# A hybrid encoder layer on one core: two small parameter loads issued later, zeroing and copies placed elsewhere, the way-in steps redistributed

## The reference, cut to what matters

```python
q, k, v, u, g_a, g_s = split(rms_norm(h) @ w_in)
# attention: 4 heads, two score maps per head
p = softmax(einsum('bqhcd,bkhcd->bhcqk', rope(q), rope(k)) * 64 ** -0.5)
w = p[:, :, 0] - lam * p[:, :, 1]
o_a = rms_norm(w @ v) * (1 - lambda_init)
# S5, both directions, 32 groups of 64 states, 16 channels each
bb = coef * (b_re + i b_im)          # discretised input matrix
x_t = ab * x_{t-1} + bb @ u_t        # scan over 256 steps
y = Re((c_re + i c_im) @ x) + d * u
```

## Time and profile before

| | |
|---|---|
| Median of 3 runs | 1339.34 us (1339.18 to 1340.71) |
| The profiled execution's own time | 1338.22 us |
| Its span in the profile | 1336.3 us |
| TensorE (PE) matmul busy | 1264.0 us (95%) |
| TensorE weight load (PEld) busy | 569.2 us (43%) |
| VectorE (DVE) busy | 373.2 us (28%) |
| ScalarE (ACT) busy | 202.1 us (15%) |
| GpSimd (POOL) busy | 111.2 us (8%) |
| Read from HBM over the span | 454.11 MB, 341 GB/s |
| Mean granted TensorE clock | 0.987 of full speed |

### The profile page before, as it was taken

The page is one execution under the profiler, slowest core; times in us unless marked ns, Lnnn a source line. Parts: engine busy times, 40 slices in busy tenths (PEclk is TensorE's granted clock), DMA queues, the critical chain, the costliest instruction groups (busy, mean ns, idle before and its releaser), DMA issues.

```text
span 1336.3 us, 15275 instructions
## 1 busy us (share of the span) xinstructions
PE 1264.0 (95%) x6167; PEld 569.2 (43%) x6167; DVE 373.2 (28%) x797; ACT 202.1 (15%) x311; POOL 111.2 (8%) x109
## 2 busy tenths in 40 slices
PE   7998899999898999999999999999999999999997
PEld 3477776777743333333333333333333332333332
DVE  6389675022123211122111211112211111221112
ACT  2121252101310111111111111111111111111111
POOL 4499110010001000000000000000000000000000
PEclk8999899999998999999999999999999999999999
DMA  8643375347954999999999999999999999999995
GB/s 229 175 133 126 102 89 175 127 158 283 354 222 167 412 427 429 428 427 428 427 429 427 429 428 429 430 427 429 427 429 430 427 430 428 428 430 427 430 427 218
DMA packets 55128, 456.83 MB, mean 342 GB/s; under 512 B 4760, under 2 KB 6880, under 8 KB 30512
## 3 DMA queue, kind: packets, MB, share of 16 engines
q1 hardware_dynamic: 51744, 449.74, 81.8%
q0 software_dynamic: 2192, 5.99, 2.7%
q10 hardware_dynamic: 1152, 0.52, 0.3%
HBM read 454.11 MB, written 1.61 MB: 341 GB/s over the span
## 4 chain that ended last, share of the span: by engine, by line
PE 62%; DMA 30%; DVE 4%; ACT 2%; issue 1%; SPq 0%; ACTq 0%; DVEq 0%
PE pt L872 17%; DMA ring<-in_w_e 16%; PE pt L912 12%; PE pt L487 7%; DMA stage<-in_w_e 6%; DMA low<-in_w_e 6%; PE pt L474 6%; PE pt L522 4%; PE pt L839 3%; PE pt L826 3%; PE pt L454 3%; PE pt L535 2%; DMA stage<-in_w_in 1%; PE pt L878 1%; ACT wi_ L950 1%
## 5 line engine op out<-in xcount | busy, mean ns | idle before, releaser
L872 PE MATMUL pt<-ring,hres 128*64 128x512 f32 x1216 | 273.1, 595 | 15.2 <-DMA ring<-in_w_e 14.9
L872 PEld LDWEIGHTS pt<-ring,hres 128*64 128x64 f32 x1216 | 84.0, 137 | 198.6 <-issue 167.0
L912 PE MATMUL pt<-ring,wi_ 128*64 128x512 f32 x640 | 141.7, 595 | 5.4 <-ACT wi_ L950 5.4
L1549 DVE TENSOR_SCALAR hnt<-pt 128x512 f32<-128x512 f32 x32 | 22.1, 692 | 308.2 <-PE pt L872 308.2
L1495 DVE COPY ct_<-ct_ 128x2 f32 (+1 forms) x33 | 5.6, 169 | 363.6 <-PE pt L872 359.1
L872 PE MATMUL pt<-stage,hres 128*64 128x512 f32 x416 | 93.9, 595 | 6.7 <-DMA stage<-in_w_e 6.7
L872 PE MATMUL pt<-low,hres 128*64 128x512 f32 x416 | 93.8, 595 | 5.0 <-DMA low<-in_w_e 5.0
L1110 ACT ACTIVATE hnt<-hnt 128x512 f32<-128x512 f32 x32 | 20.2, 630 | 477.8 <-DVE hnt L1549 477.8
L912 PEld LDWEIGHTS pt<-ring,wi_ 128*64 128x64 f32 x640 | 44.5, 137 | 89.7 <-issue 82.4
L839 PE MATMUL pt<-big,lamb 64*128 64x512 f32 x256 | 63.6, 615 | 0.7 <-ACT big L950 0.7
L474 PE MATMUL pt<-stage,hnt 128*128 128x512 f32 x128 | 58.9, 622 | 4.5 <-DMA stage<-in_w_in 4.5
(11 more groups left out here) (314 smaller groups left out, 1265.9 us busy)
## 6 DMA issues: line engine op xcount, KB each, us to landing
ring<-in_w_e SPq DMA_DIRECT2D x116, 2048.0 KB, 40.1
low<-in_w_e SPq DMA_DIRECT2D x38, 2048.0 KB, 41.0
stage<-in_w_e SPq DMA_DIRECT2D x38, 2048.0 KB, 40.0
stage<-in_w_in SPq DMA_DIRECT2D x16, 1024.0 KB, 5.6
stage<-in_w_xkv SPq DMA_DIRECT2D x8, 1024.0 KB, 5.5
stage<-in_w_mix_out SPq DMA_DIRECT2D x4, 1024.0 KB, 5.0
stage<-in_w_xq SPq DMA_DIRECT2D x4, 1024.0 KB, 5.1
stage<-in_w_xo SPq DMA_DIRECT2D x4, 1024.0 KB, 16.3
```

What stands on the lines that cost most here:

```text
L872: last = pe.matmul(pt[PC][SLOTS * g:SLOTS * (g + 1), 512 * b:512 * (b + 1)], xT[:, k % 4, k // 4], ring_slot[n][:, c:c + 512], start=(k == ...
L912: last = pe.matmul(pt[PD][SLOTS * h:SLOTS * (h + 1), 512:1024], hT[:, c, g], ring_slot[n][:, D * c + 512 * h:D * c + 512 * (h + 1)], start ...
L1549: dve.tensor_scalar(hg, pt[PC][:, 0:512], GATE_MAX, None, ALU.min).then_inc(m_g2, 1)
```

## The change

C is loaded only when the second half of slab "u" has landed, and B only when the second half of "q" has. The clears of `bsplit` and of the k halves move up behind the first norm; the rotation's temporaries move from `t3` to a free part of `ring`. The four copies into `bsplit` move from VectorE to ScalarE, behind its copy of the regrouped u. The scaling of the second map in `weigh` moves to ScalarE, behind the exponentials of its head; VectorE signals the factors (`wsc`) and waits for each scaled tile (`wsv`). The way-in steps of VectorE are t = 0 before head 0, 1 after head 0, 2 after head 1, 3 and 4 after head 2. The chunk factors come after head 3. `turn_probs(3)` comes after the second of the eight groups of way-in transposes.

```diff
@@ -371,12 +371,14 @@
                            T["norm_ffn_g"].rearrange("a (j p r) -> p (a j) r", p=P, j=W1_CHUNKS)).then_inc(s_par, 16)
 
             pool.wait_ge(S["graw"], 1)
+            pool.wait_ge(s_slot[1], 16)
             for c, n in enumerate(("ssm_c_re", "ssm_c_im")):
                 for d in range(2):
                     dst = craw[:, c, :, d * NS:(d + 1) * NS]
                     src = T[n][0, d].rearrange("(j a) h p -> (a h) j p", j=4)
                     pool.dma_start(dst, src).then_inc(s_bc, 16)
 
+            pool.wait_ge(s_slot[3], 16)
             for c, n in enumerate(("ssm_b_re", "ssm_b_im")):
                 for d in range(2):
                     pool.dma_start(braw[d * NS:(d + 1) * NS, c], T[n][0, d].rearrange("g p h -> p g h")).then_inc(s_bc, 16)
@@ -649,7 +651,6 @@
                                          s5w[:, c, 8 * j + a], start=(c == 0), stop=(c == 1))
             last.then_inc(S["kp"], 1)
             values(2)
-            turn_probs(3)
 
 
             pe.wait_ge(S["bp"], 2)
@@ -659,6 +660,8 @@
                 for i in range(8):
                     last = turn(pt[u][:, P * i:P * (i + 1)], s5b[:, 4 * r + i // 2, i % 2])
                 last.then_inc(S["ltp"], 1)
+                if r == 1:
+                    turn_probs(3)
             values(3)
 
 
@@ -987,6 +990,12 @@
             copy(vn, unit(PB, "p (t n) -> p t n", t=NT)).then_inc(S["vev"], 1)
             act.wait_ge(S["utp"], 1)
             copy(uT_[:, :], unit(PC)).then_inc(S["uta"], 1)
+            act.wait_ge(S["bsz"], 1)
+            act.wait_ge(S["bbr"], 1)
+            for c in range(2):
+                copy(bsplit[0:NS, c, :, 1], bbar[0:NS, c])
+                last = copy(bsplit[NS:P, c, :, 0], bbar[NS:P, c])
+            last.then_inc(S["bspl"], 1)
             slab_done(act, "ga0")
             act.wait_ge(S["tabp"], 1)
             copy(a1[:, 0:1024], unit(PA)).then_inc(S["gates"], 1)
@@ -1006,6 +1015,9 @@
                         i = 2 * c + t
                         act.activation(prob[:, c, t], pt[PD][:, 512 * c + L * t:512 * c + L * (t + 1)], ACT.Exp,
                                        bias=sm[:, i:i + 1], scale=DH ** -0.5, accum_out=sm[:, 8 + i:9 + i]).then_inc(S["pex"], 1)
+                act.wait_ge(S["wsc"], h + 1)
+                for t in range(NT):
+                    act.activation(prob[:, 1, t], prob[:, 1, t], ACT.Copy, scale=sm[:, 20 + t:21 + t]).then_inc(S["wsv"], 1)
 
             def copy_probs(h):
                 act.wait_ge(S["wtp"], h + 1)
@@ -1191,6 +1203,9 @@
             link(dve.tensor_copy(gains[:, 0:3 * KD], pt[PA][:, 0:3 * KD]))
             gained(0, 0, PC, hnT)
             gained(0, 1, PD, hnT)
+            dve.memset(ring[:, 20480:22528], 0.0).then_inc(S["bsz"], 1)
+            dve.memset(big[0:DH, 0:1024], 0.0)
+            dve.memset(t3[DH:P, 512:1024], 0.0).then_inc(S["kz"], 1)
 
 
             dve.wait_ge(s_par, 112)
@@ -1263,8 +1278,8 @@
             cos = con[:, C_COS:C_COS + NT * 32].rearrange("p (t i) -> p t i", t=NT)
             sin = con[:, C_SIN:C_SIN + NT * 32].rearrange("p (t i) -> p t i", t=NT)
             dve.wait_ge(s_con, 16)
-            rt1 = t3[:, 0:512].rearrange("p (c f i) -> p c f i", c=8, f=2)
-            rt2 = t3[:, 512:1024].rearrange("p (c f i) -> p c f i", c=8, f=2)
+            rt1 = ring[:, 18432:18944].rearrange("p (c f i) -> p c f i", c=8, f=2)
+            rt2 = ring[:, 18944:19456].rearrange("p (c f i) -> p c f i", c=8, f=2)
             for n, slab, u, dst in ((1, "q", PB, qn), (2, "k", PA, kn)):
                 slab_done(dve, slab)
                 for t in range(NT):
@@ -1280,9 +1295,6 @@
                         link(last)
                 last.then_inc(S["rope"], 1)
                 dve.wait_ge(S["rope"], n)
-            dve.memset(big[0:DH, 0:1024], 0.0)
-            dve.memset(t3[DH:P, 0:1024], 0.0).then_inc(S["kz"], 1)
-
 
             dve.wait_ge(S["taba"], 1)
             for c in range(2):
@@ -1298,19 +1310,17 @@
             link(dve.tensor_tensor(bbar[:, 0], tmp_v, bbar[:, 0], ALU.subtract))
             link(dve.tensor_tensor(tmp_v, braw[:, 1], cfr, ALU.mult))
             link(dve.tensor_tensor(bbar[:, 1], braw[:, 0], cfi, ALU.mult))
-            link(dve.tensor_tensor(bbar[:, 1], tmp_v, bbar[:, 1], ALU.add))
-            link(dve.memset(ring[:, 20480:22528], 0.0))
-            for c in range(2):
-                dve.tensor_copy(bsplit[0:NS, c, :, 1], bbar[0:NS, c])
-                last = dve.tensor_copy(bsplit[NS:P, c, :, 0], bbar[NS:P, c])
-            last.then_inc(S["bspl"], 1)
+            dve.tensor_tensor(bbar[:, 1], tmp_v, bbar[:, 1], ALU.add).then_inc(S["bbr"], 1)
+            dve.wait_ge(S["bbr"], 1)
 
             l8 = lam8[:, 0:128].rearrange("p (f c g) -> p f c g", f=2, c=2)
-            for lo, hi, t in ((0, NS, TC - 1), (NS, P, 0)):
-                dve.tensor_copy(l8[lo:hi, 0, 0], wpow[lo:hi, 0, t])
-                dve.tensor_copy(l8[lo:hi, 1, 1], wpow[lo:hi, 0, t])
-                dve.tensor_copy(l8[lo:hi, 0, 1], wpow[lo:hi, 1, t])
-                link(dve.tensor_scalar(l8[lo:hi, 1, 0], wpow[lo:hi, 1, t], -1.0, None, ALU.mult))
+
+            def chunk_factors():
+                for lo, hi, t in ((0, NS, TC - 1), (NS, P, 0)):
+                    dve.tensor_copy(l8[lo:hi, 0, 0], wpow[lo:hi, 0, t])
+                    dve.tensor_copy(l8[lo:hi, 1, 1], wpow[lo:hi, 0, t])
+                    dve.tensor_copy(l8[lo:hi, 0, 1], wpow[lo:hi, 1, t])
+                    link(dve.tensor_scalar(l8[lo:hi, 1, 0], wpow[lo:hi, 1, t], -1.0, None, ALU.mult))
 
             dve.wait_ge(S["laml"], 1)
             dve.wait_ge(s_par, 112)
@@ -1327,10 +1337,9 @@
 
                 dve.wait_ge(S["pex"], 4 * (h + 1))
                 link(dve.reciprocal(sm[:, 16:20], sm[:, 8:12]))
-                link(dve.tensor_scalar(sm[:, 20:22], sm[:, 18:20], st[:, 45:46], None, ALU.mult))
+                dve.tensor_scalar(sm[:, 20:22], sm[:, 18:20], st[:, 45:46], None, ALU.mult).then_inc(S["wsc"], 1)
                 for t in range(NT):
-                    link(dve.tensor_scalar(prob[:, 1, t], prob[:, 1, t], sm[:, 20 + t:21 + t], None, ALU.mult))
-                for t in range(NT):
+                    dve.wait_ge(S["wsv"], NT * h + t + 1)
                     last = dve.scalar_tensor_tensor(prob[:, 0, t], prob[:, 0, t], sm[:, 16 + t:17 + t], prob[:, 1, t],
                                                     ALU.mult, ALU.add)
                 last.then_inc(S["pwv"], 1)
@@ -1359,12 +1368,14 @@
                 dve.wait_ge(S["kse"], 1)
 
             dve.wait_ge(S["tabp"], 1)
-            for h, times in enumerate((range(0, 2), range(2, 4), range(4, WAY_IN_SPLIT), ())):
+            way_in(range(0, 1))
+            for h, times in enumerate((range(1, 2), range(2, 3), range(3, WAY_IN_SPLIT), ())):
                 row_max(h)
                 weigh(h)
                 if h == 0:
                     lag0()
                 way_in(times)
+            chunk_factors()
             for r in range(1, 8, 2):
                 dve.wait_ge(S["ltp"], r + 1)
                 dve.tensor_copy(ring[:, 8192 + 1024 * r:8192 + 1024 * (r + 1)], pt[PD][:, :]).then_inc(S["ltv"], 1)
```

More of the change, by code:

```diff
@@ L179, in build @@
             sgm bav yp ygel ytp graw yta gls osv bsv mh xqa xsp xmx xex xpn xtp xta xop xoa xh lgp lgv lex msk
-            rkp rkv gdv gdp gda cup cuv ovp ovi hn3 gfin accd rope gates qkp qka sumsq normed tokp
+            bsz bbr wsc wsv rkp rkv gdv gdp gda cup cuv ovp ovi hn3 gfin accd rope gates qkp qka sumsq normed tokp
             tokv""".split()
```

## The result

| | before | after |
|---|---|---|
| Median | 1339.26 us (1337.38 to 1340.71, 4 runs) | 1326.80 us (1323.93 to 1328.03, 4 runs) |
| Ratio | | 0.9908 (95% interval 0.9887 to 0.9929) |
| Profiled execution | 1338.22 us, span 1336.3 | 1328.03 us, span 1326.1 |

The change saves 12.5 us of the median. The profiled execution of the kernel after is the slowest of its four, 1.2 us above the median, and shows 10.2 us less span than the one before.

What follows compares the result with a forecast made beforehand. The expert-weight stream bounds the kernel and starts when TensorE frees ring slots, so TensorE savings ahead count 1:1. Terms -4.6 - 12.7 + 2.5 + 2.0 = -12.8 us give a median of 1326.5 us, range 1321.5 to 1332.

Steps and rivals of the forecast that it cites:

- Early loads: At slab "u": delaying B and C removes the 2.34 us pause and the low clock behind it; -4.6 us together.
- 0.4 us more: At the start of slab "u", late on a load: it starts earlier, a gain of 0.4 us.
- the first low stretch: First 8 records of slab "u", 5.4 us for 3.4 at low clock; assumed to stay, -6.5 together if it goes.
- Head 1: At transposing head 1's probabilities: the 9.74 us wait goes with 2.7 us margin, plus 3.0 us of low clock; -12.7 us.
- Heads 2 and 3: Before the way-in transposes: a new 3.2 us wait costs +1.6, a second wait among the groups +0.9; +2.5 us together.
- The clock: At the wait before the way-in transposes: the clock falls and slows the first groups of transposes; +2.0 us (0 to 5.9).
- The length taken from slab "u": At the way-in transposes: the low-clock stretch lasts 3.6 us, as in slab "u".
- (1): Rival: the clock stays low through all way-in transposes, costing 5.9 us instead of 2.0; 1330.4 us, chance 0.08.
- (2): Rival: head 1's probabilities come 2 us late, with a wait and perhaps low clock; 1328.5 to 1331.5 us, chance 0.1.
- (3): Rival: no gain, head 3 returns the 12.7 us or the stream does not start with TensorE; 1339 us, chance 0.04.
- (4): Rival: slower, B lands late and TensorE stands before slab "k"; 1343 us, chance 0.05.
- the 13 named as a sign: At the start of the expert stage: expert matmuls start 13 us earlier if the prediction is right.

Runs made afterwards that it cites:

- y1_waits_only: The kernel before with only the two waits ahead of the loads of C and B added; ratio 0.9973 to the kernel before.
- x1_loads_back: The kernel after without the two waits, so B and C are issued at once again; median 1331.9 us, ratio 0.9953 to the kernel before.
- steps back: The kernel after with VectorE's way-in steps placed as before (0, 1 after head 0; 2, 3 after head 1; 4 after head 2); median 1334.6 us, ratio 0.9969.
- clears back: The kernel after with clears, the four copies into split B and chunk factors on VectorE in their old places; median 1332.0 us, ratio 0.9956.
- scaling back: The kernel after with both scalings of the second map on VectorE again; median 1330.3 us, ratio 0.9948.
- x5_fill_wait: The kernel after with three unused 128x512 matmuls on TensorE in the wait before the way-in transposes; median 1324.5 us, ratio 0.9887.
- x4_probs_back: The kernel after with the transposes of head 3's probabilities before the way-in transposes again; median 1323.6 us, ratio 0.9900.
- x7_pool_step4: The kernel after with way-in step 4 moved from VectorE to POOL; median 1330.0 us, ratio 0.9929.

## Why the prediction was right, and where it was not

The median came out at 1326.8 us for 1326.5, by the mechanisms named. That the two agree to 0.3 us is luck: the four executions spread over 4 us, and the errors of the steps below partly offset each other. By its steps:

**Early loads, -4.6.** Measured -4.1 in the profile of after; -5.5 in that of y1_waits_only, where the clock stayed up, and -3.6 by its ratio. The pause (2.34 us) and the low stretch behind it went. Two steps of the term failed. "0.4 us more" for an earlier start: slab "u" starts at 12.78 to 13.69 us with the waits, at 13.07 and 12.72 without. Small pieces of C were not what held the first half. And the first low stretch, "which I leave where it is", is not a fixture: nine of twelve profiles have none, and x1_loads_back, without the waits, has none either. One error took from the gain and the other added to it.

**Head 1, -12.7.** Measured -12.9 from A to B. TensorE asks at 123.47 us, and the probabilities were ready at 120.35, a margin of 3.1 us for the 2.7 worked out. The edits hold it together: steps back, a wait of 6.44; clears back, 3.13; scaling back, 1.75. Each of the three groups is needed, and the spread of the steps most.

**Heads 2 and 3, +2.5.** The wait was predicted as 3.2 us and was 2.86, behind the instruction named. Measured at full clock (x5_fill_wait) the term is +3.0 us: from B to the way-in transposes 10.8 us for 9.4 (+1.4, predicted +1.6), and from there to C 12.1 for 10.5 (+1.6, predicted +0.9). The second part is the mis-sized one: the copy of group 0 keeps TensorE 1.60 us, and VectorE's copies catch up only 0.2 us of it (from group 2 to C 8.15 us for 8.35).

**The clock, +2.0.** Right that it falls. The size differs from execution to execution: 3.75 us in the profile of after, 1.3 and 1.7 in two others of the same work. The length taken from slab "u", 3.6 us, fits those two, where it was 3.4 us; in after it lasted from about 149.5 to 159.7, and there the step failed: it gave one length to what varies with the same work. That is most of the 2.6 us by which the profiled difference falls short of -12.8. The median does not fall short; how many of the other executions had the shorter stretch is not shown.

**Rivals.** (1), the low clock through all transposes (+5.9), did not come, though in the profile of after it came more than half way; it rose to 1.00 at 159 to 160 us in the middle of transposes. The statement of the Trainium skill (TensorE: Matmul & The Clock Gate, Part 4) that full clock does not engage for transposes is not borne out by that row. (2) had a margin of 3.1 us and none of it was used up. (3) and (4) fell with the first expert matmul at 407 us (10.6 us earlier in this profile, for the 13 named as a sign) and B's landing within 9.2 us.

What is still open: whether the lambdas' packets at 9 to 10 us delay slab "u", why the low-clock stretches at slab "u" and 261 us behind C come or not with the same work, and why that at head 3 lasted 3.4 us in two profiles and 10.2 in a third.

## What to carry to other kernels

An engine that works in a fixed order has its slack in one place and its debts in another: look for the longest idle time ahead of the first deadline (here VectorE before head 0) and move into it what stands between deadlines, before anything is sped up. When work moves to another engine, read that engine's queue at every place where it goes, not on average: the scalings delayed nothing on ScalarE for three heads and cost 1.5 us of wait and a fall of the clock in the fourth, where one reordered copy got it back. And judge a part by its own stretch of the timeline when other stretches scatter by more than it is worth.

## What the runs showed of the hardware

- The length of a wait alone does not decide on TensorE's clock. Ahead of slab "u", with the same work before and behind it, it fell after waits of 2.10, 2.55 and 2.59 us and stayed at 1.00 after nine of 1.77 to 2.87 us. At head 1, behind a gate slab, waits of 1.75 and 3.13 us left it at 1.00, while 6.44 and 9.74 us lost it, 5.2 and 2.1 us after they began. At head 3, behind the taps' 128 records of small products and the values, all seven unfilled waits of 2.23 us or more lost it, and all four of 1.19 to 1.67 us did not. Whether the work ahead of the wait makes the difference between head 1 and head 3 is not shown. The windows of y2_clears_back, with the wait of 3.13 us and that of 4.17:

```profile
125.00:126.00 1.00, 0.82 (x6) 0.80 (x7) 1.00 (x2) 0.13 (x1) 1.00 (x1) 1.00 1.04 387
...
151.00:152.00 1.00, 0.00 (x0) 0.00 (x0) 0.39 (x3) 0.64 (x2) 0.00 (x0) 0.56 0.00 0
```

- The fall can come after the wait is over. In x4_probs_back TensorE works again from 148.03 us on, and the grant goes down then:

```profile
147.00:148.00 1.00, 0.00 (x0) 0.00 (x0) 0.91 (x4) 1.00 (x3) 0.00 (x0) 1.00 0.05 14
148.00:149.00 1.00, 0.97 (x7) 0.94 (x8) 0.76 (x8) 0.58 (x2) 0.00 (x0) 0.74 0.00 0
149.00:150.00 1.00, 1.00 (x6) 1.00 (x5) 0.00 (x0) 0.38 (x1) 0.00 (x0) 0.50 0.61 94
```

- Beside a working POOL the same VectorE operation on 128x512 takes 1.43 to 1.75 us instead of 0.69 (x7_pool_step4: 1.65 at 140.10 us, 0.69 from 141.79 on, with POOL done at 141.2), and two combinations of 128x256 take 2.02 instead of 0.88; a step given to POOL lengthened those that VectorE kept.
